# VectorE multiplies and sums three pieces of the first modulation's last column block; ScalarE makes q's last high part before it issues seven DMAs

## The reference, cut to what matters

```
def ada_modulation(cond, w_ada, b_ada):
    m = jax.nn.silu(cond) @ w_ada + b_ada        # w_ada: 2048 x 12288
    return [p[:, None, :] for p in jnp.split(m, N_MOD, axis=-1)]
...
    sh1, sc1, g1, sh2, sc2, g2 = ada_modulation(cond, w_ada, b_ada)
    h = rms_norm(x, g_norm1) * (1 + sc1) + sh1
    proj = h @ w_in
    q, k, v, bg, cg, u = jnp.split(proj, ...)
```

## Time and profile before

| | us |
|---|---|
| median of 3 runs (lowest, highest) | 1527.26 (1527.1, 1527.64) |
| span of the profiled execution, first to last instruction | 1525.0 |
| what lies outside the span, against the median | 2.26 |
| TensorE busy | 1446.9 (95%) |
| VectorE busy | 602.3 (39%) |
| ScalarE busy | 255.1 (17%) |
| bytes moved, mean rate | 572.48 MB, 375 GB/s |

### The profile page before, as it was taken

The page is one execution under the profiler, slowest core; times in us unless marked ns, Lnnn a source line. Parts: engine busy times, 40 slices in busy tenths (PEclk is TensorE's granted clock), DMA queues, the critical chain, the costliest instruction groups (busy, mean ns, idle before and its releaser), DMA issues.

```text
span 1525.0 us, 18551 instructions
## 1 busy us (share of the span) xinstructions
PE 1446.9 (95%) x7856; PEld 882.0 (58%) x7856; DVE 602.3 (39%) x1019; ACT 255.1 (17%) x358; POOL 26.7 (2%) x58
## 2 busy tenths in 40 slices
PE   6999999999999999999989989999889899899998
PEld 3667788888889997435435335335335335335433
DVE  4433977978768986101301301301301301211313
ACT  4233223333233223000000000000000000000200
POOL 0000000000000000000000000000000000000000
PEclk9999999999999999999999999999999999999999
DMA  9999688777787659999999999999999999999999
GB/s 374 403 395 325 263 324 316 268 261 260 276 294 273 221 191 366 371 433 434 430 431 433 427 435 431 431 434 428 435 431 430 434 429 435 431 429 431 431 422 349
DMA packets 99263, 572.48 MB, mean 375 GB/s; under 512 B 9532, under 2 KB 54532, under 8 KB 76676
## 3 DMA queue, kind: packets, MB, share of 16 engines
q1 hardware_dynamic: 87824, 520.14, 83.5%
q0 software_dynamic: 6912, 50.33, 8.6%
q10 hardware_dynamic: 4468, 1.14, 0.3%
HBM read 565.02 MB, written 6.55 MB: 375 GB/s over the span
## 4 chain that ended last, share of the span: by engine, by line
PE 66%; DMA 24%; DVE 5%; SPq 2%; issue 2%; ACT 1%; ACTq 0%; DVEq 0%
PE psum L639 64%; DMA ring<-in_w_up 20%; DMA ring<-in_w_ada 2%; SPq L551 2%; DMA res<-in_w_ada 1%; DVE res L1618 1%; DVE w_parts L1508 1%; DMA ring<-in_w_down 1%; PE psum L649 0%; PE psum L825 0%; PE psum L1077 0%; DVE stat L1578 0%; DVE hid L1577 0%; PE psum L1047 0%; DVE mix L1581 0%
## 5 line engine op out<-in xcount | busy, mean ns | idle before, releaser
L639 PE MATMUL psum<-ring,hid 128*64 128x512 f32 x3024 | 679.9, 596 | 54.0 <-DMA ring<-in_w_up 40.2
L639 PEld LDWEIGHTS psum<-ring,hid 128*64 128x64 f32 x3024 | 240.2, 138 | 470.3 <-issue 414.3
L1944 DVE TENSOR_TENSOR hid<-psum,hid 128x512 f32<-128x512 f32 x16 | 11.1, 691 | 516.3 <-PE psum L639 516.3
L639 PE MATMUL psum<-h_parts,w_parts 128*128 128x384 f32 x1152 | 207.3, 337 | 1.3 <-DVE mix L1651 1.3
L639 PEld LDWEIGHTS psum<-h_parts,w_parts 128*128 128x128 f32 x1152 | 199.9, 188 | 5.1 <-issue 2.5
L1508 DVE TENSOR_TENSOR w_parts<-ring,w_parts 128x2048 fp32r<-128x2048 f32 x52 | 119.0, 2289 | 76.4 <-ACT w_parts L1208 76.2
L1208 ACT ACTIVATE w_parts<-ring 128x2048 fp32r<-128x2048 f32 x52 | 99.6, 1916 | 209.0 <-PE psum L639 176.9
L639 PE MATMUL psum<-w_parts,h_parts 128*128 128x512 f32 x432 | 103.9, 395 | 2.8 <-DVE w_parts L1508 1.5
L639 PE MATMUL psum<-ring,early 128*32 128x512 f32 (+4 forms) x694 | 96.4, 536 | 7.8 <-DMA ring<-in_w_ada 6.0
L639 PEld LDWEIGHTS psum<-w_parts,h_parts 128*128 128x128 f32 x432 | 79.5, 188 | 28.5 <-issue 10.3
L639 PEld LDWEIGHTS psum<-early,mix 128*128 128x128 f32 x768 | 86.6, 192 | 9.0 <-issue 9.0
(11 more groups left out here) (216 smaller groups left out, 754.0 us busy)
## 6 DMA issues: line engine op xcount, KB each, us to landing
ring<-in_w_up SPq DMA_DIRECT2D x30, 4096.0 KB, 23.2
ring<-in_w_gate SPq DMA_DIRECT2D x28, 4096.0 KB, 30.4
ring<-in_w_down SPq DMA_DIRECT2D x26, 4096.0 KB, 30.0
ring<-in_w_ada POOLq DMA_DIRECT2D x48, 1024.0 KB, 7.5
ring<-in_w_in SPq DMA_DIRECT2D x36, 1024.0 KB, 8.3
ring<-in_w_ada SPq DMA_DIRECT2D x28, 768.0 KB, 15.6
res<-in_w_ada SPq DMA_DIRECT2D x16, 1024.0 KB, 5.7
ring<-in_w_out SPq DMA_DIRECT2D x16, 1024.0 KB, 5.8
```

The lines of the kernel that those rows point to most:

```text
L639: return nc.tensor.matmul(out, lhsT, rhs, start=start, stop=stop, skip_group_check=True)
L1944: tt(by_row, bank[1][:, :].rearrange("p (b a) -> p a b", a=4), by_row, ALU.mult).then_inc(act_ready, 1)
```

## The change

Three of block 2's pieces, 33, 34 and 35, are no longer multiplied by TensorE. VectorE multiplies each of their two chunks by the conditioning value of its row (one value for each partition, for each of the two conditioning vectors) and sums the products in two tiles of 128 x 1024 (`spared_sums`). That is `piece_add(n)`, four instructions for each piece. They stand ahead of `lo_part(5)`, between `lo_part(5)` and `lo_part(6)`, and ahead of `h_block(2)`. `start_sums` on TensorE sums the two tiles over the partitions into bank 0, behind piece 39. The loads of pieces 37, 38 and 39 wait for VectorE's sums of the pieces in their buffers, 33, 34 and 35, in place of TensorE's count. The counts that VectorE and GpSimd wait for go down accordingly. `hi_part(7)` moves ahead of ScalarE's seven DMAs. The idle work behind piece 15 goes.

```
+SPARED = [33, 34, 35]
 PIECE_FREE = ...
-    [24, 25, 26, 28] + list(range(33, 37))
+    [24, 25, 26, 28] + [33, 0, 0, 0]
...
-             (6, 2): [32, 33], (7, 2): [34], (8, 2): [35, 36], (9, 2): [37], (10, 2): [38, 39]}
+             (6, 2): [32], (8, 2): [36], (9, 2): [37], (10, 2): [38, 39]}
...
+        spared_sums = [hid[:, 2 * D // 2:3 * D // 2], hid[:, 3 * D // 2:4 * D // 2]]
...
                 if PIECE_FREE[n]:
                     sp.wait_ge(w_used, PIECE_FREE[n])
+                if n - len(SPARED) - 1 in SPARED:
+                    sp.wait_ge(spared_added, 4 * (SPARED.index(n - len(SPARED) - 1) + 1))
...
-            pool.wait_ge(w_used, len(PIECES))
+            pool.wait_ge(w_used, PIECE_ENDS[-1] - len(SPARED) + 1)
...
+            def start_sums():
+
+                width = BLOCKS[2][1]
+                for n in range(2):
+                    for j in range(4):
+                        cols = slice(j * width // 2, (j + 1) * width // 2)
+                        last = mm(bank[0][32 * j:32 * j + 32, 0:width // 2], add_rows_of[:, 1 - n:33 - n], spared_sums[n][:, cols], False, n == 1)
+                last.then_inc(w_used, 1)
...
-                if n >= IDLE_FROM:
+                if n in range(IDLE_FROM, PIECE_ENDS[0] - 1):
                     idle_work(IDLE_PIECE)
...
+                    if (k, t) == (10, 2):
+                        pe.wait_ge(spared_added, 4 * len(SPARED))
+                        pe.wait_ge(ones_set, 3)
+                        start_sums()
...
             h_block(2, None, None)
+            hi_part(7)
 
             a.dma_start(kc, ...)          (and six more)
...
-            hi_part(7)
             hi_part(8)
...
-                v.wait_ge(w_used, PIECE_ENDS[b])
+                v.wait_ge(w_used, PIECE_ENDS[b] - (len(SPARED) - 1 if b == 2 else 0))
...
+            def piece_add(n):
+
+                width = BLOCKS[2][1]
+                v.wait_ge(piece_in[PIECE_SEM[n]], piece_landed(n))
+                rows = piece_buf(n).rearrange("p (m k n) -> p m k n", m=2, n=width)
+                for kk, k in enumerate(PIECES[n][1]):
+                    for cc in range(2):
+                        done = 4 * SPARED.index(n) + 2 * kk + cc
+                        sums = spared_sums[cc].rearrange("p (m n) -> p m n", m=2)
+                        if done < 2:
+                            ts(sums, rows[:, :, kk, :], cond[:, k, cc:cc + 1], None, ALU.mult).then_inc(spared_added, 1)
+                        else:
+                            v.wait_ge(spared_added, done - 1)
+                            stt(sums, rows[:, :, kk, :], cond[:, k, cc:cc + 1], sums, ALU.mult, ALU.add).then_inc(spared_added, 1)
+
+            piece_add(SPARED[0])
             lo_part(5)
+            piece_add(SPARED[1])
             lo_part(6)
+            piece_add(SPARED[2])
             h_block(2, None, None)
```

More of the change, by code:

```diff
@@ L332, in build @@
         piece_in = [sem(f"piece_in{n}") for n in range(B_BUFS)]
-        w_used = sem("w_used")
+        w_used, spared_added = sem("w_used"), sem("spared_added")
         start_rows_out, start_turned = sem("start_rows_out"), sem("start_turned")
@@ L683, in piece @@
                         at = (j // 2 * len(ks) + kk) * width + j % 2 * width // 2
-                        last = mm(bank[0][32 * j:32 * j + 32, 0:width // 2], cond[:, k, :], piece_buf(n)[:, at:at + width // 2], k == 0, k == KC - 1)
+                        last = mm(bank[0][32 * j:32 * j + 32, 0:width // 2], cond[:, k, :], piece_buf(n)[:, at:at + width // 2], k == 0, b < 2 and k == KC - 1)
+                last.then_inc(w_used, 1)
[5 more added lines that the diff above has]
+                        last = mm(bank[0][32 * j:32 * j + 32, 0:width // 2], add_rows_of[:, 1 - n:33 - n], spared_sums[n][:, cols], False, n == 1)
                 last.then_inc(w_used, 1)
```

## The result

The changed kernel's median is 1538.33 us (1537.04 to 1538.59, 4 runs), against 1527.2 beside it: a ratio of 1.0072, 95% interval 1.0061 to 1.0084. The forecast was 1535.5 with a range of 1531.8 to 1538.8. The span of the profiled execution (its own time 1537.04) is 1535.4 us, 10.4 us more than before.

What follows compares the result with a forecast made beforehand. TensorE, busy 95% of the span, and full DMA engines were taken to bound the q projection. Stand +8.0, gap -1.5 and clock +1.7 gave +8.2 us: span 1533.2, median 1535.5, range 1531.8 to 1538.8.

Steps and rivals of the forecast that it cites:

- Idle work, taken as 0: Idle work behind piece 15, 1.38 us: an earlier turn is waited away at piece 31; 0, ends 0 and -1.2 us.
- VectorE's prices: `piece_add` instructions of 128 x 1024: multiply 0.7 us, multiply and add 1.25 us; 13.9 us in all.
- The new wait, steps 1 to 6: Loads 37 to 39 wait for VectorE's sums; load 39 issues at 122.0, lands at 127.0, TensorE stands from 118.0: +8.0 us.
- The gap: TensorE's idle gap of 1.49 us ahead of chunk 14 goes when `hi_part(7)` starts earlier: -1.5 us.
- The clock: Behind TensorE's stand before piece 39, one dip of the granted clock: 1.7 us, ends 0 and 3.4.
- Rival A: Stand before piece 39 without the clock dip: +6.5 us, 1533.8; chance 0.15.
- "As before, 8.0 us later" for what follows: `h_block(2)`, six matmuls and the turn run unchanged, 8.0 us later; the delay should reach the end undiminished.
- The sum: +8.0 - 1.5 + 1.7 = +8.2 us on the span of 1525.0: 1533.2; median 2.26 above the span: 1535.5.
- The range: 1531.8 to 1538.8: below, Rival A with quick landing, +4.9; above, forecast with two dips and some of Rival B.
- Rival B: Longer stand: loads queue at landing, multiply without its faster rate, two clock dips; +11 to +13, about 1539; chance 0.12.
- Rivals C and E: C: later stages soak up the delay, about 1528, 0.05. E: only ScalarE's part counts, 1525.8, 0.03 shared with Rival D.
- Rival D: Load 39 out before about 112 us, no stand at piece 39: -3.4 us, 1523.9; chance 0.03 together with E.

Runs made afterwards that it cites:

- Experiments 2 and 7: 2: changed kernel with piece 35's sums ahead of `lo_part(6)`, 1531.48 us; 7: kernel before with load 39 made to wait for `lo_part(6)`, 1534.31 us.
- experiment 1: Kernel before with only ScalarE's part of the change, `hi_part(7)` ahead of the seven DMAs: 1525.50 us, ratio 0.9993.
- experiment 4: Changed kernel with 40 identity multiplications on TensorE ahead of piece 39, measured in two sets: 1541.0 and 1536.13 us.
- add_first: Changed kernel with `piece_add(35)` moved ahead of `lo_part(6)`: 1531.48 us, ratio 1.0031 against the kernel before.
- dmas_first: Changed kernel with the seven DMAs ahead of `hi_part(7)` again: 1540.56 us, ratio 1.0083 against the kernel before.
- busy_wait_again: Second measurement of the changed kernel with 40 identity multiplications on TensorE ahead of piece 39: 1536.13 us.
- late_39: Kernel before with one added wait, the load of piece 39 waiting for `lo_part(6)`, no added work: 1534.31 us, ratio 1.0045.
- scalar_only: Kernel before with only `hi_part(7)` moved ahead of ScalarE's seven DMAs: 1525.50 us, ratio 0.9993.
- five_no_vector: Kernel before with `hi_part(7)` ahead of the seven DMAs and a fifth piece buffer for block 2, all eight pieces on TensorE: 1525.50 us.
- five_bufs: Changed kernel with `piece_add(35)` ahead of `lo_part(6)` and five piece buffers for block 2 in place of four: 1524.39 us, ratio 0.9985.
- busy_wait: First measurement of the changed kernel with 40 identity multiplications on TensorE ahead of piece 39: 1541.0 us.

## Why the forecast was right in kind and short in size

By TensorE's timeline, changed kernel against before:

| | start before | start after | later by |
|---|---|---|---|
| chunk 6 of q | 91.70 | 91.75 | 0.05 |
| turn of block 2 | 122.36 | 133.32 | 10.96 |
| first event of the next modulation | 139.61 | 148.77 | 9.16 |
| wait for VectorE's mix in the convolution | 250.22 | 260.29 | 10.07 |
| end of the span | 1525.0 | 1535.4 | 10.4 |

- **Idle work, taken as 0: right, and for the reason given.** The turn of block 0 and q's first chunk start 0.3 to 0.4 us earlier, and piece 31 gives it back, waiting for its load (its weight load waits 0.86 us for the DMA, 0.48 before); the timeline of the changed kernel:

```profile
86.33 0.85 PE L643 MATMUL psum<-ring,early 128*32 128x384 f32 x8 [0.17 <-DMA ring<-in_w_ada]
```

- **VectorE's prices: right.** 1.28 us by its record, 1.22 from start to start, for a multiply-and-add of 1024 (I took 1.25), 0.75 by its record and 0.66 from start to start for a multiply (0.7). 13.6 us in all against 13.9.
- **The new wait, steps 1 to 6: right.** Issues at 105, 111.8 and 122.4 against the forecast's 104.9, 112.1 and 122.0. Unit 6's high part started at 113.36, not 112.8; piece 39 landed 5.2 us after the first issue (5.0). Piece 39 and the sums would end at 129.5 at full clock, +8.7 where I had +8.0. Experiments 2 and 7 show the cause from both sides.
- **The gap: -1.8 us, not -1.5**, in the changed kernel (10.96 to 9.16) as in experiment 1.
- **The clock: right in kind, sized too low.** 2.3 us, not 1.7 (experiment 4). I had taken the price from two stretches in which TensorE still worked a part of the time. Here it resumed at the low clock and stayed there to about 132.6, longer than those. Rival A, the stand without the dip, is out. The Trainium skill ("TensorE: Matmul & The Clock Gate", Part 1) says that the array is throttled when idle and that activity releases the throttle. The trace agrees: the granted clock fell to 0.50 inside the stand, at about 122.4 us, and rose 5 us after work began.
- **"As before, 8.0 us later" for what follows: 0.9 us too good.** Between 242 and 260 us TensorE lost 0.9 us more. The gap that VectorE's mix ends is 1.91 us and was 1.29. In the chain of the changed kernel a 1024 KB load of VectorE's later sums takes 7.0 us where the same one took 5.15. The same gap is 2.29 in add_first, 2.11 in dmas_first and 2.33 in busy_wait_again, 1.29 in late_39, 1.18 in scalar_only, 1.23 in five_no_vector, and absent in five_bufs and in busy_wait (which has 1.13 us at 242.56, ended by a DMA). late_39 comes there 7.75 us later than the kernel before and still has 1.29, so lateness alone does not set it. What does was not tried, and this part of the loss stays unexplained. From 260 us to the end it is 0.3 more.
- **The sum.** On the span: 8.2 forecast, +0.7 stand, +0.6 clock, -0.3 gap, +0.9 and +0.3 later stages = 10.4, as measured. The median of the four runs is 1.3 us above the profiled execution; 1538.3. That is 2.93 above its span, where I had added 2.26: another 0.7.
- **The range held by 0.5 us, and in part by luck.** The upper end, 1538.8, was made of a second dip of the clock and some of rival B. There was one low stretch, dearer by 0.6, and the rest came from the stand, the later stages and the median's distance from the span. The lower end was added up wrongly: a landing 0.46 and unit 6 0.5 us sooner take 1.0 from A's +6.5, which gives +5.5 and not +4.9.
- **Rival B** (a longer stand, about 1539) has the nearer number, 0.7 us off against the forecast's 2.8, but not the cause: the multiply kept its faster rate, there were no two dips, and the stand's part was 0.7 us over the forecast. Rivals C and E are out: TensorE is still 10.07 us late at 260 us, and the end of the span 10.4.
- **Rival D** (faster if load 39 is out before 112) was the right condition: five_bufs issues it behind the sums of piece 34 and is faster. In the changed kernel the condition isn't met.

## What to carry to other kernels

When work moves from one engine to a less busy one, look for what the old engine's progress released: a buffer that is handed back in another engine's order can be handed back much later, although neither engine is short of time. Follow the loads that wait in the same queue behind it too. Two cures were shown here: put the releasing work ahead of the work that waits (-6.9 us), or give the loads a buffer whose release does not hang on it (another 7 us).

## What was not expected of the hardware

- DMA issues on ScalarE run beside its activations. In the changed kernel `hi_part(7)` runs from 137.64 to 139.54 while issues stand at 137.39, 137.93, 138.54, 139.02. Only an activation that is queued behind the issues waits for them.
- The same 1024 KB load took 5.2 us from the first issue with three loads behind it in the changed kernel and 7.1 us in late_39, also with three behind it. In both the DMA engines had little to do just before (share 0.24 in 116 to 121 us in late_39, 0.05 in 116 to 118 and 0.00 in 118 to 122 in the changed kernel). No run here tells why.
- The filled stand kept TensorE's granted clock at 1.00 (117 to 131 us, both executions that were profiled), and useless multiplications were enough for it.
